# A decoder step on one core: shifted rows added to kept rows by accumulating DMAs, key products two steps later, first pages over four steps

## What is computed

```
xn   = rms_norm(x)
proj = xn @ w_in                       # 1024 x 3328: q, k (rotated), v, and 1792 columns p_rw
# time mixing, on the 1792 columns:
p_prev = concatenate([shift0, p[:-1]])  # the row before, or the stored shift row of a sequence
ps     = p + (p_prev - p) * mu          # everything after this reads ps
...                                     # low-rank gates, a chunked recurrence over 64-row chunks
# attention: prompt rows causal, sample rows over 512 cached rows (4 pages of 128) and their own
h    = x + concat(o_attention, o_time_mixing) @ w_out
hn   = rms_norm(h)
q    = hn @ peer_wq                     # 8 heads x 2 halves x 128
s    = q . sub_keys                     # 128 scores for each half
# top 16 of each half, top 16 of the 256 sums, softmax -> 128 experts of 16384 for each row
y    = h + sum over the 128 experts of gate * gelu(u_e . hn) * v_e
out  = rms_norm(y)
```

## Time and profile before

| | us |
|---|---|
| median of 3 runs | 3897.75 (3897.39 to 3907.1) |
| the profiled execution | 3912.04 |
| its span, first to last instruction | 3910.2 |
| fill, up to the first expert gather | 694 |
| slots, from there to the end | 3216 |

### The profile page before, as it was taken

One profiled execution on the slowest core, in us unless ns is written; L12 is line 12 of the kernel. 1 busy time (PEld: TensorE's weight loads), 2 busy tenths in 40 slices (PEclk: granted clock), 3 DMA queues, 4 the chain that ended last, 5 costly groups with the idle time before them and its releaser, 6 DMA issues. The chain is left out here.

```text
span 3910.2 us, 57756 instructions
## 1 busy us (share of the span) xinstructions
PE 2888.9 (74%) x21998; PEld 1520.7 (39%) x21998; DVE 2558.8 (65%) x5772; ACT 1287.6 (33%) x3599; POOL 1359.8 (35%) x1190
## 2 busy tenths in 40 slices
PE   8889899676776677777857776777676758877554
PEld 3446546332533244334423443433352325534111
DVE  1431762788498759866885788578847875435954
ACT  1211211434243433434343435243423233322222
POOL 1000000443343434333433443244324466533453
PEclk9999999877887887777878787888886677667566
DMA  7436336999999999999999999999999999999998
GB/s 252 158 109 216 121 140 225 382 419 420 418 412 420 410 419 410 397 411 418 412 397 420 417 412 384 421 411 419 381 409 386 357 382 392 374 403 397 419 403 352
DMA packets 253415, 1418.23 MB, mean 363 GB/s; under 512 B 27249, under 2 KB 45185, under 8 KB 103889
## 3 DMA queue, kind: packets, MB, share of 16 engines
q0 software_dynamic: 163232, 1162.26, 72.9%
q1 hardware_dynamic: 89904, 252.26, 17.2%
HBM read 1367.96 MB, written 46.46 MB: 362 GB/s over the span
## 5 line engine op out<-in xcount | busy, mean ns | idle before, releaser
L989 POOL DMA_INDIRECT pe_buf<-in_experts,pe_idx x1088 | 1274.4, 1171 | 2382.6 <-PE pe_psO L1400 1661.3
L2229 DVE CUSTOM_DVE_ANT_0 pe_buf<-pe_buf,pe_hnR 128x1024 f32<-128x1024 f32 x1088 | 1315.6, 1223 | 689.4 <-DMA pe_buf<-in_experts,pe_idx 660.9
L1400 PE MATMUL pe_psO<-pe_buf,pe_Z 128*32 128x256 f32 x8704 | 831.7, 476 | 521.3 <-ACT pe_Z L1673 489.6
L1667 ACT ACTIVATE pe_gelu<-pe_dot 128x1 f32<-128x1 f32 x1088 | 219.2, 201 | 1599.3 <-DVE pe_dot L2229 1555.7
L1400 PEld LDWEIGHTS pe_psO<-pe_buf,pe_Z 128*32 128x32 f32 x8704 | 211.4, 122 | 1155.2 <-ACT pe_Z L1673 865.4
L1382 PE MATMUL pe_psH<-pe_hn,pe_pick 128*128 128x512 f32 x544 | 420.8, 866 | 40.4 <-ACT pe_hnR L1649 36.3
L1023 PE MATMUL ip_B<-ip_w,ip_xT 128*128 128x512 f32 (+1 forms) x1008 | 426.6, 574 | 5.3 <-DMA ip_w<-in_w_in 5.3
L1673 ACT ACTIVATE pe_Z<-pe_gl,pe_gelu 128x8 f32<-128x8 f32 x1088 | 327.3, 301 | 48.0 <-PE pe_psO L1400 3.2
L1333 PE MATMUL pe_B<-pe_mix,op_wq 128*128 128x128 f32 (+1 forms) x2304 | 300.9, 294 | 6.1 <-DMA op_wq<-in_peer_wq 4.7
L1333 PEld LDWEIGHTS pe_B<-pe_mix,op_wq 128*128 128x128 f32 x2304 | 290.0, 208 | 38.5 <-issue 32.6
L1023 PEld LDWEIGHTS ip_B<-ip_w,ip_xT 128*128 128x128 f32 x1008 | 189.5, 194 | 197.8 <-issue 193.0
(11 more groups left out here) (340 smaller groups left out, 3570.8 us busy)
## 6 DMA issues: line engine op xcount, KB each, us to landing
op_wq<-in_peer_wq SPq DMA_DIRECT2D x36, 2048.0 KB, 15.0
ip_w<-in_w_in SPq DMA_DIRECT2D x18, 2048.0 KB, 8.4
op_w<-in_w_out SPq DMA_DIRECT2D x9, 2560.0 KB
pe_buf<-in_experts,pe_idx POOLq DMA_INDIRECT x1088
op_w<-in_w_out SPq DMA_DIRECT2D x9, 1024.0 KB
tm_ps<-scratch_moved_rows SPq DMA_DIRECT2D x8, 896.0 KB
tm_p<-scratch_kept_rows SPq DMA_DIRECT2D x8, 896.0 KB
out_p_all<-ip_o SPq DMA_DIRECT2D x27, 256.0 KB, 5.8
```

The lines of the kernel that those rows point to most:

```text
L989: pool.indirect_dma_start(buf[b][:], None, T["experts"], bass.IndirectOffsetOnAxis(ap=idx[:, t % 2, h * NJ + j:h * NJ + j + 1], axis=0)).t ...
L1400: last = nc.tensor.matmul(psO[32 * x:32 * x + 32, j // 4, :], Z[:, n % NZ, 24 - 8 * turn:56 - 8 * turn], buf[home[n]][:, D + x * QUART:D + ...
L1667: nc.scalar.activation(gelu[:, col:col + 1], dot[:, col:col + 1], ACT.Gelu_apprx_tanh).then_inc(f["gelu_done"], 1)
L2229: nc.vector.tensor_tensor_reduce(buf[b][:, 0:D], buf[b][:, 0:D], hnR[:, n // PH % 2, :], 1.0, 0.0, ALU.mult, ALU.add, dot[:, n % (NBUF + E ...
```

## The change

The change has three parts.

1. **The sum is made in DRAM.** POOL adds each unit's moved rows to the kept rows with a DMA that accumulates (accum_op), two steps after the unit is projected, when SP's stores of it have landed. Each such DMA also waits until all earlier ones have landed (`mixed`). The first stands behind the end of POOL's constants. SP then loads one tensor, kept_rows, straight into ps (load_p) at step 25, when the tile's adds have landed. DVE's add L1816 and the loads into p are gone, and the readers of ps wait for the load. For the sample tile there are two adds for each unit (7 rows of each sequence, and the first rows from moved_shift), and its state and constants are loaded at step 29.
2. **The products with the keys** move from steps 31 and 32 to 33 and 34, and the score copies from 32 and 33 to 35 and 36. OP_STEPS goes from 35 to 38, which shifts the merged order of the fill and the steps for each slot a little.
3. **The first 16 page gathers** are split into four groups, at steps 6, 7, 8 and 9 of the sample tile's attention, and DVE's copies into QB go from step 10 to step 7.

```diff
-OP_STEPS = 35
+OP_STEPS = 38
...
+    def added_of(units):
+        return 16 * sum(1 if t < LAST else 2 for t, n in UNITS[:units] if n >= NV)
+
+    def mixed_of(t):
+        return added_of(last_unit(t) + 1)
...
                     if i == IP_FIRST + 2:
                         sp.wait_ge(at["lam_dots"], 1)
-                        sp.wait_ge(ip["edge_stored"], 32)
                         load_p(0)
...
             def load_p(t):
 
                 R = rows_of(t)
...
+                sp.wait_ge(ip["mixed"], mixed_of(t))
+                sp.dma_start(ps[0:R], kept_rows[rows(t, R), :]).then_inc(s["p_in"], 16)
...
                         sp.wait_ge(op["hn_stored"], 16 * (t + 1))
-                        if t + 1 < LAST:
-                            load_moved(t + 1)
+                        load_p(t + 1)
...
-                    if k == 29 and t < LAST:
+                    if k == 29 and t + 1 == LAST:
                         sp.wait_ge(op["chunk_done"], NC * t + NC - 1)
-                        if t + 1 < LAST:
-                            load_kept(t + 1)
-                        else:
-                            load_p(t + 1)
+                        load_sample_consts()
...
+                    if 2 <= i < len(IP) + 2:
+                        kind, g, q_ = IP[i - 2]
+                        if kind == "unit" and q_ == 1 and UNITS[g][1] >= NV:
+                            add_moved(g)
+                    yield
+
+            def add_moved(g):
+
+                t, n = UNITS[g]
+                cols = slice((n - NV) * IG, (n - NV) * IG + cols_of(n))
+                for i in range(2):
+                    pool.wait_ge(ip_stored[i], stored_of(g + 1, i))
+                if t == 0:
+                    pool.wait_ge(ip["edge_stored"], 32)
+                if added_of(g):
+                    pool.wait_ge(ip["mixed"], added_of(g))
+                if t < LAST:
+                    pool.dma_start(kept_rows[rows(t), cols], moved_rows[t * P:(t + 1) * P, cols], accum_op=ALU.add
+                                   ).then_inc(ip["mixed"], 16)
+                    return
+                kept = kept_rows[rows(LAST, SROWS), cols].rearrange("(b s) n -> b s n", s=ST)
+                moved = moved_rows[1 + SEQ:1 + SEQ + SROWS, cols].rearrange("(b s) n -> b s n", s=ST)
+                pool.dma_start(kept[:, 1:ST, :], moved[:, 0:ST - 1, :], accum_op=ALU.add).then_inc(ip["mixed"], 16)
+                pool.dma_start(kept[:, 0, :], moved_shift[:, cols], accum_op=ALU.add).then_inc(ip["mixed"], 16)
...
-                    if k == SB_LEAD - 1:
+                    if k == SB_LEAD - 4:
                         pool.wait_ge(at["pidx_ready"], 1)
                         pool.wait_ge(s["state_stored"], 32)
-                        for b in range(2):
-                            pages_of(kp, "cache_k", kp_in, b)
-                            pages_of(vp, "cache_v", vp_in, b)
+                        pages_of(kp, "cache_k", kp_in, 0)
+                    if k == SB_LEAD - 3:
+                        pages_of(vp, "cache_v", vp_in, 0)
+                    if k == SB_LEAD - 2:
+                        pages_of(kp, "cache_k", kp_in, 1)
+                    if k == SB_LEAD - 1:
+                        pages_of(vp, "cache_v", vp_in, 1)
...
-                            pe.wait_ge(s["dve_part"], ND * t + MIXED)
+                            pe.wait_ge(s["p_in"], 16 * (t + 1))
...
-                    if k in (31, 32):
+                    if k in (33, 34):
...
-                    if k in (32, 33):
-                        for n_ in (2 * k - 64, 2 * k - 63):
+                    if k in (35, 36):
+                        for n_ in (2 * k - 70, 2 * k - 69):
...
-                            dve.wait_ge(s["p_in"], 32 + 32 * t if t < LAST else 32 * PT + 160)
-                            nc.vector.tensor_tensor(ps[0:R], ps[0:R], p[0:R], ALU.add).then_inc(s["dve_part"], 1)
...
-                    yield
-                for k in range(SB_STEPS * (SB - 1) + SB_LONG):
-                    if k == 0:
+                    if k == 7:
                         dve.wait_ge(at["turned"], 2 * NT)
```

36 lines of the change are left out of this document (11 added, 25 removed).

## The result

| | median of the runs | range | profiled execution (its span) |
|---|---|---|---|
| before | 3897.6 us | 3897.4 to 3907.1 | 3912.0 us (3910.2) |
| after | 3961.6 us | 3952.3 to 3962.7 | 3961.9 us (3960.2) |

The changed kernel is slower: ratio 1.0153, 95% interval 1.0131 to 1.0174. That is 64 us between the medians, and 60 us by the ratio with its interval of 51 to 68; plus 18.6 was forecast, and 3946 us was the upper end. The two profiled executions are 50 us apart, since that of before lies 14 us above its own median.

What follows compares the result with a forecast made beforehand. The fill was taken as bound by PE, the slots from 694 to 3060 us by bytes. Terms 29.7 + 1.2 - 12.3 + 0 + 0 = 18.6 us over the median of 3897.75 gave 3916 us, range 3893 to 3946 us.

Steps and rivals of the forecast that it cites:

- part 2 at zero: Keys' products two steps later: waits hide behind the gathers in the slots; zero, bounds minus 2 and plus 2 us.
- the pages: Sample tile's page gathers split: POOL's 5 to 8 us wait for pidx offsets the win; 0, bounds minus 5 and plus 4.
- Tile 0's chain: In the fill, seven serial adds 4.5 us apart delay PE by 27.2 us, plus 2.5 us for its clock: 29.7 us.
- The rivals of a short and a long chain: Tile 0's adds 2.7 to 3.5 us apart, 3903 to 3909 us (0.23), or 6.5 to 8.6, 3931 to 3949 us (0.18).
- The first gather's 1.2 us: At the fill's end, POOL's two more add issues delay the first expert gather by 1.2 us, up to 6 us.
- The bytes: In the slots, 5.05 MB less is loaded for tiles 3 to 8: minus 12.3 us, bounds minus 10 and minus 16.
- The long chain: Adds at a fraction of the copy's rate, a (issue to issue) 6.5 to 8.6 us; 3931 to 3949, up to 3954 us; 0.18.
- The forecast: The prediction's main case for the whole kernel, 3910 to 3930 us, given a chance of 0.47.
- The rival with the page's price: Tile 0's seven adds take 18 to 22 us, whole change plus 5 to plus 10 us; the short chain's case, 0.23.

Runs made afterwards that it cites:

- e2_keys_back: The changed kernel with the keys' products back at steps 31 and 32 and OP_STEPS 35; ratio 1.0042 to the kernel before.
- e14_fill_dense: Kernel before with the keys' products later, OP_STEPS 38, old slots kept in the windows, but the fill's order from the planner's full cost; ratio 1.0008.
- e5_keys_old_places: Kernel before with the keys' products later and OP_STEPS 38, planner's cost per output projection step at 35/38, so time mixing and attention keep old slots; ratio 0.9994.
- e3_keys_alone: Kernel before with only the keys' products at steps 33 and 34, score copies at 35 and 36, and OP_STEPS 38; ratio 1.0104.
- e7_sum_early: Kernel before with only the sum made in DRAM, and moved_shift stored early so that tile 0's adds do not wait behind it; ratio 0.9952.
- e9_pair_apart: Kernel before with OP_STEPS 38, the three added steps empty, and time mixing's steps 54 to 58 one slot later in six windows; ratio 1.0071.
- e15_pair_57_58: Kernel before with OP_STEPS 38, and time mixing's steps 54 to 57 one slot later in six windows, so 57 and 58 share slot 50; ratio 1.0040.

## Why the prediction was wrong

The direction was right, the size was not: plus 64 us (60 by the ratio) against plus 18.6. The step that failed is part 2 at zero; the pages are over their bound, and the fill grew more than I had it even without part 2. Point by point:

- **Tile 0's chain** was right. I had seven adds 4.5 us apart, the load at 166.7 us and PE 27.2 us late with 2.5 us for the clock. It was 4.9 us on average from 135.98 to 165.23 us (29.25 us over six steps), the load at 168.44 and PE 28.9 us late. In e2_keys_back the fill grew by another 3 us behind the stall, at a granted clock of 0.67 from 130 to 180 us against 0.98. The rivals of a short and a long chain are out. For this part of the sum I had 30.9 us at the first gather, and without part 2 it was 37.9: 29.3 at PE's first matmul, the 3 behind the stall, 3 more between 250 and 500 us of the kernel before for which I have no cause, and the rest around the last stores and adds.
- **The first gather's 1.2 us** for the last adds held in itself: 1.5 us stand between the last add and the gather. The fill's order, which I put inside part 2's plus 2, was 8.9 us in the trace of e14_fill_dense, and 1.0 us in the change by e2_keys_back.
- **The bytes** were right in kind and a little large: 8.8 to 10.3 us in the six windows against 12.3. In the changed kernel part 2's loss covers them, so that the stretch became longer and the term seemed to have failed. What I had missed is the sample tile's load, now one transfer and four steps earlier, worth 8 to 12 us: I had given its pieces 1 or 2 us and had not priced the step.
- **Part 2 at zero is the step that failed.** I looked at the waits ahead of the products, which say that the products can move, and e5_keys_old_places shows that they can. I had named the shift of the plan and bounded it by 2 us from nothing but the fill. Its price is about 1% by e3_keys_alone, some 41 us; in its trace 33 us are in the windows and 8 in the fill. The row that could have warned me was there: DVE waits for PE's state product 66.8 us in all, so that two engines hand work to and fro inside these slots, and a planner that pairs two of these steps makes one wait inside a slot.
- **The pages** went as argued, POOL's wait of 6.26 us inside my 5 to 8. The drought became shorter too (longest wait of DVE for a gather 12.2 us after, 14.7 before), and it didn't help. The value, though, is not zero but 0.17 to 0.21%, some 7 to 8 us, over the upper bound of plus 4. I had set the six gathers that come earlier against POOL's wait as if nothing were lost with it; the 8 to 9 us more from the 820th to the 860th gather say that it is.

With parts 2 and 3 at the prices measured for each alone, and the sample tile's earlier load at minus 10, the sum is 18.6 + 41 + 7 - 10 = 57 us, against 60 measured by the ratio, with 51 to 68 for its interval. That is an estimate after the fact, and it is partly luck: the fill was 7 us more than its term and the bytes 2 to 3 us less, so without part 2 the same terms give 18.6 + 7 - 10 + 7 + 3 = 26 us, where e2_keys_back measured 0.42%, 16 us.

Three slips of the prediction changed little. The long chain's times by its own formula, 7a - 12.9, end at 3945 and 3950 us, not at 3949 and 3954. The forecast and the long chain lie wholly above 3909.4 us, so the chance of slower should have been at least 0.65, not 0.58. And in the slices DVE does reach 9 behind slice 7, in three of them.

The rival with the page's price, from the Trainium skill, "DMA: Bandwidth & Descriptors", section "Anatomy of one DMA", put an add at 2.6 to 3.2 us. The two sizes in the kernel after disagree in the slope: 3.2 us for 128 KB and 4.4 us for 256 KB are 2.0 us and 9.2 us per MB, where the page's 436 GB/s would be 2.3 us per MB. With a second read counted, an estimate by that page is 4.6 us per MB, half of it. The fixed part, about 2.0 us by this fit, would agree, but it hangs on two medians: in e7_sum_early they are 3.5 and 4.3 us, which makes 2.7 us and 6.1 us per MB. That an add is slower than the page's copy holds either way.

## What to carry to other kernels

A constant that feeds a planner is a change to every stream that the planner places: before such an edit compare what shares a slot before and after, above all pairs of steps between which two engines hand work to and fro, and price it from the waits between these engines. When an operation leaves an engine for a DMA, look for the one place where nothing runs ahead of it, and cut the serial waits there first; here part 1 is 0.5% faster with one 56 KB store early and, by the 0.69% between the two, some 0.2% slower with it late. And a single trace is compared with a sibling experiment's, not with one that lay off its own median.

## What was not expected of the hardware

- An accumulating DMA from DRAM to DRAM landed 4.4 us after its issue for 256 KB and 3.2 us for 128 KB, against 5.6 and 3.7 us for SP's plain stores; GpSimd spent 0.8 us on issuing one. Several in flight overlap: from the first of the seven that tile 0 needs to the load behind them it took 13.5 us, and 32.5 with one after the other.
- TensorE ran the same 166 matmuls with 12.91 us busy at a granted clock of 1.00 and with 20.21 us at 0.61, in two windows of one trace (e9_pair_apart). In the change the slow stretch at 0.55 came behind 14 us with 12.18 busy and 14 us with 7.93, where before these were 12.62 and 10.47. TensorE's own wait there grew by 0.44 us and the stretch by 6 us, so the price came mostly in work at the lower clock; what makes the clock fall was not tried by itself, and in e15_pair_57_58 it fell in two windows of six with that wait as before.
- 14 us of VectorE's work in a stretch with a DMA share of 1.00 could be taken out or put back without any effect on the time (0.9952 and 0.9950), while in the second window its wait for the second update, 8.7 us longer, came with 10.9 us lost at gathers 48 to 64.
